# A hybrid recurrent trunk on one core: the chunked recurrence inserted two token tiles at a time

## The reference

```python
x = x + 0.5 * swiglu(rmsnorm(x, n1), f1g, f1u, f1d)
proj = rmsnorm(x, nmix) @ w_in               # q, f, i, g, xr, yr, gA, gB: each 1024 wide
...
def step(S, inp):                            # hgrn2_chunked, per head, state 128 x 128
    qi, gi, ki, vi = inp
    b = jnp.cumsum(gi, axis=2)
    bl = b[:, :, -1:, :]
    qe = qi * jnp.exp(b)
    ke = ki * jnp.exp(-b)
    inter = jnp.einsum('bhck,bhkv->bhcv', qe, S)
    A = jnp.where(mask, jnp.einsum('bhck,bhsk->bhcs', qe, ke), 0.0)
    intra = jnp.einsum('bhcs,bhsv->bhcv', A, vi)
    S_new = jnp.exp(bl[:, :, 0, :])[..., None] * S + jnp.einsum(
        'bhsk,bhsv->bhkv', ki * jnp.exp(bl - b), vi)
    return S_new, inter + intra
...
x = x + m @ w_out
x = x + 0.5 * swiglu(rmsnorm(x, n3), f2g, f2u, f2d)
```

## Time and profile before

| | |
|---|---|
| median of three runs | 2431.41 us (2430.89 to 2431.72) |
| span of the profiled execution | 2428.6 us |
| PE busy | 2415.6 us, 99% |
| DVE busy | 1739.7 us, 72% |
| ACT busy | 1300.1 us, 54% |
| recurrence of the first head | from 748 to 776 us |
| recurrence of the seven steady heads | 22 us out of every 51, from 803 to 1131 us |

### The profile page before, as it was taken

The page is one execution under the profiler, slowest core; times in us unless marked ns, Lnnn a source line. Parts: engine busy times, 40 slices in busy tenths (PEclk is TensorE's granted clock), DMA queues, the critical chain, the costliest instruction groups (busy, mean ns, idle before and its releaser), DMA issues.

```text
span 2428.6 us, 51528 instructions
## 1 busy us (share of the span) xinstructions
PE 2415.6 (99%) x19220; PEld 2400.9 (99%) x19220; DVE 1739.7 (72%) x2921; ACT 1300.1 (54%) x2206; POOL 171.2 (7%) x204
## 2 busy tenths in 40 slices
PE   9999999999999999999999999999999999999998
PEld 8999999999999999999999999999999999999998
DVE  8767767677689888887777775442676777777777
ACT  5355555555558676676666664211434555555554
POOL 0011111111120000000000000000200111111110
PEclk9999999999999999999999999999999999999999
DMA  4355555555541343333322235332023555555556
GB/s 144 106 123 121 121 121 121 122 121 121 135 182 54 95 114 81 88 97 100 109 90 87 69 138 178 140 131 87 18 103 88 123 122 122 122 122 122 122 123 197
DMA packets 137270, 278.34 MB, mean 115 GB/s; under 512 B 67024, under 2 KB 71632, under 8 KB 136656
## 3 DMA queue, kind: packets, MB, share of 16 engines
q1 hardware_dynamic: 114128, 192.39, 24.3%
q0 software_dynamic: 23040, 84.55, 18.4%
HBM read 154.80 MB, written 114.77 MB: 111 GB/s over the span
## 4 chain that ended last, share of the span: by engine, by line
PE 96%; DVE 2%; ACT 1%; DMA 1%; issue 0%; SPq 0%; DVEq 0%; ACTq 0%
PE banks L154 31%; PE banks L155 31%; PE banks L156 31%; PE banks L1819 1%; PE banks L1840 1%; PE banks L1850 1%; PE banks L1848 0%; PE banks L1854 0%; DMA x_sum<-f_snap 0%; DVE y L247 0%; DVE f_blk_f L504 0%; DMA raw<-w_slabs 0%; DVE f_blk_lo L528 0%; DVE x L1122 0%; ACT f_blk_hi L520 0%
## 5 line engine op out<-in xcount | busy, mean ns | idle before, releaser
L154 PE MATMUL banks<-f_blk_hi,f_u_hi 128*128 128x258 f32 x2496 | 706.7, 283 | 0.6 <-DVE f_blk_lo L528 0.4
L155 PE MATMUL banks<-f_blk_lo,f_u_hi 128*128 128x258 f32 x2496 | 705.6, 283 | 0.0
L156 PE MATMUL banks<-f_blk_hi,f_u_lo 128*128 128x258 f32 x2496 | 704.8, 282 | 0.0
L154 PE MATMUL banks<-mix_blk_hi,mix_u_hi 128*128 128x258 f32 x1808 | 515.0, 285 | 0.4 <-ACT mix_snap L1466 0.3
L155 PE MATMUL banks<-mix_blk_lo,mix_u_hi 128*128 128x258 f32 x1808 | 511.0, 283 | 0.0
L156 PE MATMUL banks<-mix_blk_hi,mix_u_lo 128*128 128x258 f32 x1808 | 510.2, 282 | 0.0
L154 PEld LDWEIGHTS banks<-f_blk_hi,f_u_hi 128*128 128x128 f32 x2496 | 471.4, 189 | 2.2 <-issue 1.1
L156 PEld LDWEIGHTS banks<-f_blk_hi,f_u_lo 128*128 128x128 f32 x2496 | 471.1, 189 | 0.0
L155 PEld LDWEIGHTS banks<-f_blk_lo,f_u_hi 128*128 128x128 f32 x2496 | 470.9, 189 | 0.2
L154 PEld LDWEIGHTS banks<-mix_blk_hi,mix_u_hi 128*128 128x128 f32 x1808 | 342.1, 189 | 1.0 <-issue 0.8
L155 PEld LDWEIGHTS banks<-mix_blk_lo,mix_u_hi 128*128 128x128 f32 x1808 | 341.6, 189 | 0.1
(11 more groups left out here) (306 smaller groups left out, 4378.3 us busy)
## 6 DMA issues: line engine op xcount, KB each, us to landing
raw<-w_slabs SPq DMA_DIRECT2D x220, 512.0 KB, 3.5
x_sum<-f_part POOLq DMA_DIRECT2D x126, 516.0 KB, 7.7
x_sum<-f_snap POOLq DMA_DIRECT2D x18, 516.0 KB, 10.2
x_sum<-x POOLq DMA_DIRECT2D x16, 516.0 KB, 5.8
x<-x_sum SPq DMA_DIRECT2D x16, 516.0 KB, 8.4
sg_kept<-sgt SPq DMA_DIRECT2D x8, 1032.0 KB, 5.7
sgs<-sg_kept SPq DMA_DIRECT2D x16, 516.0 KB, 4.5
x_kept<-x SPq DMA_DIRECT2D x1, 4128.0 KB, 12.1
```

The source lines that it names most:

```text
L154: pe.matmul(out, wh, xh, start=start, stop=False, skip_group_check=chained)
L155: pe.matmul(out, wh, xl, start=False, stop=False, skip_group_check=chained)
L156: return pe.matmul(out, wl, xh, start=False, stop=stop, skip_group_check=chained)
```

## The change

A head has five steps, a = 0 to 4, after halves 2, 4, 6, 8 and 10 (`CORE_STEPS`). Step a updates with tiles 2a - 1 and 2a, makes the outputs of tiles 2a - 2 and 2a - 1, and the scores of tiles 2a and 2a + 1; steps 2 and 3 make four sample rows' products each, half of them in bank 5 and half in bank 4 (bank 7 in the first head). Masks and output copies take 128x256 at once. In the first head keys are turned two tiles at a time, the first tile alone before step 0. There the outputs of steps 2 and 3 are announced together with the second sample product, and all four additions of step 3 stand in the step, where two of them stood behind the low parts before. The removed lines of the rewritten functions are left out below; they stand above.

```diff
+CORE_STEPS = (1, 3, 5, 7, 9)
...
+def core_tiles(a):
+    return [n for n in (2 * a - 1, 2 * a) if 0 <= n < TILES]
+def sample_bank(g, first):
+    return 5 if g % 2 == 0 else 7 if first else 4
+def first_keys(pe, k, s, tiles):
+    for n in tiles:
+        at = slice((n % 2) * P, (n % 2 + 1) * P)
+        pe.transpose(k.bank[4][:, at], s.ke[:, n * P:(n + 1) * P], k.ident[:, :]).then_inc(s.turned, 1)
+def core_tensor(pe, k, s, h, a, first=False):
+    def scores():
+        if first and a == 0:
+            pe.wait_ge(s.vm_ready, 1)
+        wait(pe, s.sc_used, h * 8 + 2 * a)
+        if a == 3:
+            pe.wait_ge(s.ss_new, h * 8 + 4)
+        for n in (2 * a, 2 * a + 1):
+            tok = slice(n * P, (n + 1) * P)
+            last = pe.matmul(k.bank[5][:, (n % 2) * P:(n % 2 + 1) * P], s.ke[:, tok], s.qe[:, tok], start=True,
+                             stop=True, skip_group_check=True)
+        if a >= 2:
+            if a == 2:
+                pe.wait_ge(s.sample, h * 2 + 2)
+            for g in (2 * a - 4, 2 * a - 3):
+                pe.wait_ge(s.vm_ready, h * 7 + (4 + g))
+                samples = pe.matmul(k.bank[sample_bank(g, first)][:, 2 * P:4 * P], s.kst[0:DEC_ROWS, :],
+                                    s.vm[0:DEC_ROWS, 2 * g:2 * g + 2, :], start=True, stop=True, skip_group_check=True)
+                if g % 2 == 0:
+                    last = samples
+                    if first:
+                        last.then_inc(s.sc_ready, 2)
+        if a < 2 or not first:
+            (samples if a >= 2 else last).then_inc(s.sc_ready, 2)
+        else:
+            samples.then_inc(s.o_ready, 2)
+    def updates():
+        tiles = core_tiles(a)
         if first:
+            pe.wait_ge(s.kt_moved, MOVED // TILES * (tiles[-1] + 1))
+        elif a == 0:
             pe.wait_ge(s.kt_moved, h * MOVED + MOVED)
+        if a in (0, 2):
+            pe.wait_ge(s.v_moved, h * (2 * MOVED) + (a // 2 + 1) * MOVED)
+        if a:
+            pe.wait_ge(s.u_used, h * 8 + tiles[0])
+        for n in tiles:
+            at = slice((n % 2) * P, (n % 2 + 1) * P)
+            last = pe.matmul(k.bank[6][:, at], s.kt[:, n, :], s.v[:, n, :], start=True, stop=True,
+                             skip_group_check=True)
+        last.then_inc(s.u_ready, len(tiles))
+    def outputs():
+        wait(pe, s.o_used, h * 9 + 2 * a - 2)
+        pe.wait_ge(s.sc_used, h * 8 + 2 * a)
+        if first and a > 2:
+            pe.wait_ge(s.ss_new, 4 * (a - 2))
+        for n in (2 * a - 2, 2 * a - 1):
+            o = k.bank[7][:, (n % 2) * P:(n % 2 + 1) * P]
+            if n:
+                pe.wait_ge(s.state, h * 13 + (2 * n - 1))
+                pe.matmul(o, s.s[n % 2][:, :], s.qe[:, n * P:(n + 1) * P], start=True, stop=False,
+                          skip_group_check=True)
+            last = pe.matmul(o, s.v[:, n, :], s.sc[:, n % 2, :], start=n == 0, stop=True, skip_group_check=True)
+        if a == 4:
             pe.wait_ge(s.ss_new, h * 8 + 8)
             for b in range(DEC):
+                last = pe.matmul(k.bank[7][:, 2 * P + b:2 * P + b + 1], s.ss[:, b, :], s.qe[:, SEQ + b:SEQ + b + 1],
+                                 start=True, stop=True, skip_group_check=True)
+        if a in (1, 4) or not first:
+            last.then_inc(s.o_ready, 3 if a == 4 else 2)
+    if a == 0:
         pe.wait_ge(s.ke_ready, h * 1 + 1)
         pe.wait_ge(s.qe_ready, h * 1 + 1)
+    updates()
+    if a:
+        outputs()
+    if first and a < 4:
+        first_keys(pe, k, s, range(2 * a + 1, min(2 * a + 3, TILES)))
+    if a < 4:
+        scores()
...
+    if n in CORE_STEPS:
+        a = CORE_STEPS.index(n)
+        for m in core_tiles(a):
+            act.wait_ge(s.u_ready, h * 8 + (core_tiles(a)[-1] + 1))
+            if m >= 2:
+                act.wait_ge(s.state, h * 13 + (2 * m - 4 if m > 2 else 1))
+            act.activation(s.ue[m % 2][:, :], k.bank[6][:, (m % 2) * P:(m % 2 + 1) * P], ACT.Identity,
+                           scale=s.el[:, m:m + 1]).then_inc(s.u_used, 1)
+        if first and a:
+            core_out(act, k, s, a)
+        if first and a < 4:
+            for m in range(2 * a + 1, min(2 * a + 3, TILES)):
+                core_key(act, k, s, m)
...
+    if n in CORE_STEPS:
+        a = CORE_STEPS.index(n)
+        if a:
+            dve.wait_ge(s.o_ready, h * 9 + (9 if a == 4 else 2 * a))
+            if not first:
+                dve.tensor_copy(s.qe[:, (2 * a - 2) * P:2 * a * P], k.bank[7][:, 0:2 * P]).then_inc(s.o_used, 2)
+            if a == 4 and not first:
+                dve.tensor_copy(s.qe[:, SEQ:T], k.bank[7][:, 2 * P:2 * P + DEC]).then_inc(s.o_used, 1)
+        for m in core_tiles(a):
+            dve.wait_ge(s.u_used, h * 8 + (m + 1))
+            added = s.ue[m % 2][:, :]
             if m:
+                whole = s.s_out if m == 7 else s.s[2]
+                dve.wait_ge(s.state, h * 13 + (2 * m - 1))
+                if m == 7:
+                    wait(dve, s.pstate_stored, h * 16)
+                dve.scalar_tensor_tensor(whole[:, :], s.s[m % 2][:, :], s.el[:, m:m + 1], added, ALU.mult, ALU.add)\
+                    .then_inc(s.pstate_ready if m == 7 else s.state, 1)
+                added = whole[:, :]
+            if m < 7:
+                if m:
+                    dve.wait_ge(s.state, h * 13 + 2 * m)
+                dve.tensor_scalar(s.s[(m + 1) % 2][:, :], added, s.el[:, 9 + m:10 + m], None, ALU.mult)\
+                    .then_inc(s.state, 1)
+        if a < 4:
+            wait_apart(dve, s.sc_ready, h * 8 + (2 * a + 2), s.dve_passed)
+            dve.copy_predicated(s.sc[:, :, :].rearrange("p a b -> p (a b)"), k.mask[:, :, :].rearrange("p a b -> p (a b)"),
+                                k.bank[5][:, 0:2 * P]).then_inc(s.sc_used, 2)
...
-    if 4 <= n < (7 if first else 8):
-        samples_add(dve, k, s, h, n)
-def samples_add(dve, k, s, h, n):
+    if n in CORE_STEPS[2:4]:
+        for g in (n - CORE_STEPS[2], n - CORE_STEPS[2] + 1):
+            samples_add(dve, k, s, h, 4 + g, first)
+def samples_add(dve, k, s, h, n, first):
     dve.wait_ge(s.ss_loaded, h * 16 + 16)
+    if first and n % 2:
+        dve.wait_ge(s.o_used, n - 1)
     for b in (2 * n - 8, 2 * n - 7):
         dve.scalar_tensor_tensor(s.ss[:, b, :], s.ss[:, b, :], s.el[:, 16 + b:17 + b],
-                                 k.bank[5][:, (1 + b % 2) * P:(2 + b % 2) * P],
+                                 k.bank[sample_bank(n, first)][:, (2 + b % 2) * P:(3 + b % 2) * P],
...
-            if 1 <= half <= 12:
-                core_tensor(pe, k, s, j - 1, half - 1, first)
+            if first and half == 1:
+                pe.wait_ge(s.ke_ready, 1)
+                first_keys(pe, k, s, (0,))
+            if half - 1 in CORE_STEPS:
+                core_tensor(pe, k, s, j - 1, CORE_STEPS.index(half - 1), first)
...
-                if hf == 8:
-                    samples_add(dve, k, s, h, 7)
...
-    k.mid.sc = [r.put(f"sc{n}", [P, P], F32) for n in range(2)]
+    k.mid.sc = r.put("sc", [P, 2, P], F32)
+    k.mask = r.put("mask", [P, 2, P], U8)
```

109 lines of the change are left out of this document (12 added, 97 removed).

## The result

| | before | after |
|---|---|---|
| median of the runs, us | 2430.43 (2429.15 to 2431.72, 10 runs) | 2435.68 (2434.39 to 2438.26, 10 runs) |
| span of the profiled execution, us | 2428.6 | 2433.4 |
| mean granted clock in it | 0.999 | 0.998 |

A forecast was written before the change was run, and what follows sets the result against it. TensorE, busy 99% of the span, was taken as the bound, so only time between matmuls counted. Terms -1.40 - 0.26 + 2.34 + 2.95 - 0.23 - 0.83 made +2.6 us on 2431.41: 2434.0 us, range 2431.0 to 2437.0.

The forecast's parts named there:

- A switch costs nothing: On TensorE, switching between the stream and the recurrence takes no time; fewer insertions gain 0 to 0.4 us, taken as 0.
- Joined operations are worth nothing: In steady heads, wider masks and output copies save 0.6 us of VectorE a head, worth nothing beside the matmuls.
- Steady heads, -1.40: In steady heads, TensorE's 0.22 us wait for the sample additions goes and nothing is late next: minus 1.4 us.
- The slack of 1.5 us: In steady heads, VectorE finishes its work after a step's outputs at least 1.5 us before TensorE needs it.
- The rival with a wait in each head: A steady head's step becomes too long for the two halves, so TensorE waits seven times; chance 0.06.
- First scores, -0.26: At the first head's start, the first scores move behind the copy they waited for: minus 0.26 us.
- The pauses, +2.34 and +2.95: In the first head, TensorE waits before T1 and T4 for low parts queued behind steps 2 and 3: 2.34 and 2.95 us.
- Behind it, -0.83: Behind the first head's pauses, TensorE arrives later, so two waits for ScalarE's run (0.34 and 0.49) go: minus 0.83 us.
- The end of the range that keeps both waits: Behind the first head, both late waits for ScalarE stay: term 0 in place of -0.83, so +0.8 us.
- The clock, a rival at 0.05: TensorE's clock falls in a pause, costing 1.8 us: one fall makes 2435.8 us, two 2437.6; chance 0.05.

The follow-up runs named there:

- the clean pair of runs: Kernel before with the two-tile form in steady heads only: masks and output copies joined, 2429.03 us, or split into 128x128 instructions, 2429.13 us.
- the run that has this part alone: Two-tile form in the steady heads only, first head keeping the ten one-tile insertions of the kernel before; 2429.03 us, ratio 0.9994.
- the run with both moved: Changed kernel with T1's last low part and T4's last two moved ahead of the steps that held them up, first head; 2429.72 us, ratio 0.9998.
- the kernel with everything split: Changed kernel with every joined mask and output copy done again as two 128x128 instructions; 2437.38 us, ratio 1.0030.
- the longer pause in before: Kernel before with 15 dependent writes on VectorE ahead of T4's last two low parts in the first head; 2438.06 us, ratio 1.0030.
- T4's pause alone: Changed kernel with only T1's last low part moved ahead of step 2 in the first head; 2433.41 us, ratio 1.0014.
- T1's pause alone: Changed kernel with only T4's last two low parts moved ahead of step 3 in the first head; 2433.36 us, ratio 1.0012.

## Why the prediction was right, and where it was wrong

The forecast of a small loss within the range holds; the size was off by 2.65 us, half of the whole. The absolute time was off by only 1.7 us (2434.0 forecast, 2435.68 measured), and that it is nearer is luck: the sum was added to a median of three runs, 2431.41, and the ten runs of before have 2430.43. By its steps:

- **A switch costs nothing.** Confirmed: in the steady heads the distances inside an insertion are 0.11 a record, and the 0.10 to 0.21 us per head is the wait alone. With 35 insertions fewer in the steady heads nothing else was won.
- **Joined operations are worth nothing.** Confirmed by the clean pair of runs (2429.13 split, 2429.03 joined). The joined mask was priced at 0.34 us and takes 0.34 (772.07 to 772.41). The Trainium skill's advice on larger tiles ("VectorE: DVE Perf Modes", the TRN2 errata) is true of VectorE's busy time here, which fell, and says nothing of a time that TensorE sets.
- **Steady heads, -1.40.** Measured -1.18 in the trace, 1.5 us in the medians of the run that has this part alone. The slack of 1.5 us was right as well. The mask between the outputs at 871 and those at 875.64 (timeline of VectorE after) ends at 873.99, with 0.14 for the hop at 874.13:

```profile
873.54 0.45 DVE L2037 COPY_PREDICATED sc<-mask,banks 128x256 f32<-128x256 uint8 x1
```

The rival with a wait in each head falls.
- **First scores, -0.26.** Measured -0.19: the wait went, a restart of 0.07 came.
- **The pauses, +2.34 and +2.95.** Measured 2.40 and 3.01, and both gone when the low parts stand ahead of the step. This is the step that the forecast rested on, and it was right to 0.06 us each, which is the price of a multiply followed by a dependent scale-add: 0.39 (771.09 to 771.49), where I had taken 0.33. (In the six steady heads from 817 to 1080 us the same pair takes 0.32; why it takes longer in the first head and in the last is open.)
- **Behind it, -0.83.** This term was mis-sized: measured -0.13. I let both late waits go because TensorE would arrive 0.67 later. But ScalarE's run also waits for TensorE. Its last weight part stands on a product (timeline of ScalarE after):

```profile
781.03 0.39 ACT L1966 ACTIVATE qe<-banks 128x256 f32<-128x256 f32 x1 [1.50 <-PE banks L1885]
781.31 0.17 ACT L1968 ACTIVATE qe<-banks 128x8 f32<-128x8 f32 x1
781.37 0.63 ACT L1435 ACTIVATE mix_u_hi<-mix_sum 128x512 fp32r<-128x512 f32 x1
782.52 0.63 ACT L1435 ACTIVATE mix_u_hi<-raw 128x512 fp32r<-128x512 f32 x1 [0.52 <-PE banks L156]
```

The last of them is held for 0.52 us by a product that stands behind the later update and output. The copy at 781.03 comes as forecast, 4.5 us after T4 got going once the 1.6 of the slow clock is taken off; but from it to the start of ScalarE's take (L2366 at 787.48) are 6.45 us, where before has 5.69 (775.23 to 780.92) and the run with both moved, in which TensorE is not later, 5.81. So lateness of TensorE goes round through ScalarE and comes back. I had measured the distance from the earlier trace rows to the end of the run and treated the run as ScalarE's own. The end of the range that keeps both waits was the right one.
- **The clock, a rival at 0.05.** It came true on top of the forecast, +1.6 us. The mechanism and, nearly, the price of one fall (1.8) were right, the chance was not. I had argued that no pause of 2 to 3 us stands in the stream of before, and set the chance as if that were evidence against a fall; it meant that the trace could not say. The row at the kernel's start was the only one that bore on it, and it spoke for a fall. A forecast of two pauses of 2 to 3 us should have held one fall as at least an even case: 2434.0 plus 1.6. By the Trainium skill ("TensorE: Matmul & The Clock Gate", "What's actually happening") throttled is the state that activity lifts, and here the trace agrees: behind the pause the clock fell, and with TensorE busy again, from 774.88 on, it rose at 778.8.

Together: 0.7 from the late waits and 1.6 from the clock, 0.1 from the pauses, 0.2 from the steady heads and 0.1 from the scores make the 2.7 us between +2.6 and the +5.3 of the account.

What stays open: why a pause of 2.3 us is followed by a fall in most executions and not in all, and why the second fall in the kernel with everything split lasted so much longer than all others. Neither was tried further. Nor do the traces show why the longer pause in before cost 4.2 us beyond its own length in the median.

## What to carry to other kernels

When work is put into fewer and larger steps, look first at what stands behind a step in the queue of each engine and doesn't depend on it: here three low parts of 0.6 us each, ordered behind a step of twice the length, cost 5 us, and ordered ahead of it they brought no pause. Moving an operation in a queue moves everything it frees too, the buffer of the next transfer above all. And on a TensorE that was never idle before, pauses like these (2.3 us and up) should be priced with the slower clock behind them, and not by their own length alone.

## What the runs showed of the hardware

- Around a pause of TensorE of 2.33 us or more, in a stream with next to no gap before it, the granted clock fell from its level of 2.4 GHz to 1.2 GHz in all profiled executions that had such a pause: once each behind 2.33 and 2.94 us where they stand alone, once for both in the changed kernel, at 4.04 and 4.16, and twice in the kernel with everything split. A fall cost 1.6 us in most (17 records with 0.1 us more each), 1.4 where it began inside the pause; one cost 4.6. Behind 1.20 us, and behind 1.02 us, it did not fall.
- It need not fall at once: in the changed kernel it fell 0.5 us after TensorE had started again (774.88, 775.4), with T4's pause alone 0.7 us after (772.03, 772.7), and in the kernel with everything split 0.9 and 1.5 us after (767.62, 768.5; 777.30, 778.8). With T1's pause alone it was down by the third matmul, and at 4.04 us before TensorE had started again (773.7, 774.17).
- Of the two pauses in the changed kernel, at 766.84 and 774.88, only the second was followed by a fall; in another execution, with the kernel split, each was.
- A write of 128x128 on VectorE that waits for the one before it through a semaphore takes 0.26 us from one to the next. A scale-add behind a multiply that it depends on comes 0.39 us after it in the first head and in the last, and 0.32 in the six between, where the multiply itself lasts 0.29 in all.
